# A two-layer transformer in float32 on one core: squares of the norms summed inside the stage in front, mixers with every convolution tap on VectorE and their first tiles in plain float32

## The reference, cut to what matters

```python
def rmsnorm(x, g):
    xf = xf * lax.rsqrt(jnp.mean(xf * xf, axis=-1, keepdims=True) + EPS)
    return xf.astype(x.dtype) * g
def modulate(x, shift, scale):
    return rms_norm(x) * (1 + scale) + shift
...
def second_block(x, mem, ...):
    for l in range(DEPTH):
        xn = rmsnorm(x, norm_mix[l])
        proj = xn @ w_in[l]                                # 1024 -> 2560
        u_pool, u_conv, u_diff, u_sc, u_mem = jnp.split(proj, IN_SPLITS, axis=-1)
        y_pool = pool_mixer(u_pool, pool_w[l], pool_scale[l])
        y_conv = conformer_conv(u_conv, ...)               # a * sigmoid(gate), 31 taps, layernorm, silu, @ pw
        y_diff = diff_attention(u_diff, ...)
        y_sc = short_conv(u_sc, sconv_w[l])
        y_mem = memory_attention(u_mem, mem, ...)          # kv = rmsnorm(mem, mem_g) @ w_kv
        x = x + rmsnorm(cat, group_norm) @ w_out[l]
        x = x + peer_ffn(rmsnorm(x, norm_ffn[l]), ...)
```

## Time and profile before

| | |
|---|---|
| median of 3 runs | 3560.04 us (3558.72 to 3570.94) |
| the profiled execution | 3564.15 us |
| its span | 3562.8 us |
| mean granted clock of PE | 0.944 of full |
| busy | PE 91%, PEld 78%, DVE 58%, ACT 47%, POOL 6% |

### The profile page before, as it was taken

How to read it: one execution, slowest core, us unless ns; L and a number is a source line. 1 busy time by engine, 2 the same in 40 slices (tenths; PEclk the granted TensorE clock), 3 DMA queues, 4 the chain that set the end, 5 groups by cost and what they waited for, 6 DMA issues and landing times.

```text
span 3562.8 us, 51089 instructions
## 1 busy us (share of the span) xinstructions
PE 3245.5 (91%) x19360; PEld 2768.5 (78%) x19360; DVE 2063.8 (58%) x4132; ACT 1664.8 (47%) x3572; POOL 221.6 (6%) x290
## 2 busy tenths in 40 slices
PE   7998999998899777996899999987699779999999
PEld 4745677786699766985689999987598658999998
DVE  2233433335665665598666666656558876666665
ACT  2244322223654335419755555543451685555554
POOL 0021000000200160000000000006100000000000
PEclk9999899997999787999999999978699999999999
DMA  5402344432156322440355555543053115655554
GB/s 207 177 1 83 128 174 166 151 109 72 48 181 179 108 78 65 149 160 1 105 185 185 187 185 188 185 137 106 12 178 131 65 36 184 189 184 184 189 185 153
DMA packets 135059, 479.91 MB, mean 135 GB/s; under 512 B 15520, under 2 KB 17440, under 8 KB 134048
## 3 DMA queue, kind: packets, MB, share of 16 engines
q1 hardware_dynamic: 132944, 471.26, 40.6%
q10 hardware_dynamic: 1872, 5.38, 0.4%
HBM read 475.53 MB, written 1.05 MB: 134 GB/s over the span
## 4 chain that ended last, share of the span: by engine, by line
PE 84%; DVE 8%; issue 4%; ACT 3%; DMA 1%; SPq 0%; ACTq 0%; DVEq 0%
PE psum L706 14%; PE psum L708 14%; PE psum L707 14%; PE psum L2370 7%; PE psum L2371 7%; PE psum L2372 7%; PE psum L2292 6%; PE psum L2216 4%; PE psum L557 3%; PE psum L999 2%; PE psum L354 1%; PE psum L571 1%; DVE conv_part L1457 1%; DVE w_lo L248 1%; PE psum L1009 1%
## 5 line engine op out<-in xcount | busy, mean ns | idle before, releaser
L248 DVE TENSOR_TENSOR w_lo<-raw,w_hi 128x512 fp32r<-128x512 f32 x1472 | 1005.9, 699 | 821.1 <-ACT w_hi L239 793.7
L239 ACT ACTIVATE w_hi<-raw 128x512 fp32r<-128x512 f32 x1472 | 894.8, 625 | 882.3 <-PE psum L708 495.8
L706 PE MATMUL psum<-x_hi,w_hi 128*128 128x256 f32 x2096 | 604.8, 289 | 30.7 <-DVE w_lo L248 23.4
L707 PE MATMUL psum<-x_lo,w_hi 128*128 128x256 f32 x2096 | 600.6, 287 | 0.0
L708 PE MATMUL psum<-x_hi,w_lo 128*128 128x256 f32 x2096 | 597.2, 285 | 0.0
L706 PEld LDWEIGHTS psum<-x_hi,w_hi 128*128 128x128 f32 x2096 | 401.9, 192 | 43.6 <-DVE w_lo L248 25.7
L2370 PE MATMUL psum<-w_hi,wt_hi 128*128 128x512 f32 x1024 | 407.3, 398 | 6.5 <-DVE wt_lo L2428 6.5
L707 PEld LDWEIGHTS psum<-x_lo,w_hi 128*128 128x128 f32 x2096 | 404.0, 193 | 8.2
L2371 PE MATMUL psum<-w_lo,wt_hi 128*128 128x512 f32 x1024 | 407.0, 397 | 0.0
L2372 PE MATMUL psum<-w_hi,wt_lo 128*128 128x512 f32 x1024 | 407.0, 397 | 0.0
L708 PEld LDWEIGHTS psum<-x_hi,w_lo 128*128 128x128 f32 x2096 | 406.8, 194 | 0.0
(11 more groups left out here) (315 smaller groups left out, 4652.4 us busy)
## 6 DMA issues: line engine op xcount, KB each, us to landing
raw<-in_v SPq DMA_DIRECT2D x256, 512.0 KB, 4.2
raw<-in_u SPq DMA_DIRECT2D x190, 512.0 KB, 3.4
raw<-in_mod_w SPq DMA_DIRECT2D x96, 512.0 KB, 4.2
raw<-in_w_gate_up SPq DMA_DIRECT2D x88, 512.0 KB, 4.8
u_raw<-in_u SPq DMA_DIRECT2D x66, 512.0 KB, 3.5
raw<-in_w_in SPq DMA_DIRECT2D x40, 512.0 KB, 4.0
raw<-in_w_down SPq DMA_DIRECT2D x32, 512.0 KB, 3.6
raw<-in_w_peer SPq DMA_DIRECT2D x32, 512.0 KB, 4.2
```

The source lines that it names most:

```text
L239: self.nc.scalar.activation(self.hi[:, m % 4, :], self.half(m), ACT.Copy).then_inc(self.rounded[m % 4], 1)
L248: self.nc.vector.tensor_tensor(self.lo[:, m % 4, :], self.half(m), self.hi[:, m % 4, :], ALU.subtract).then_inc(self.ready[m % 4], 1)
L706: pe.matmul(out[:, 0:width], hi[:, w], x_hi, start=(c == 0), stop=False)
L707: pe.matmul(out[:, 0:width], hi[:, w], x_lo, start=False, stop=False)
```

## The change

It has three parts.

1. **Squares within the stage in front.** For 8 norms (the four between the halves of the first block's layers and at its end, both mixers' and both PEER norms) ACT squares all chunks, DVE adds squares 0 to 6 into one buffer as they come, and PE sums the total and chunk 7's square alone (`tensor_total`): 2 chunks' worth of matmuls instead of 8. For 6 of them (`early=True`) the squares and adds stand inside the stage in front, after the tile that made the chunk. The mixers' norms wait for each chunk by itself but stand after that stage, and the memory has a norm of its own.
2. **Mixers.** All 31 taps on DVE, spread over the tiles of `first`, `mem_kv` and `second`; no conv on POOL, no join. The gate is a Sigmoid and one product. Tiles 4, 5, 2, 3 of w_in and the 4 memory tiles are plain float32 products straight from `raw` (`PlainProjection`). The memory's root, inverse and spread, the convolution's mean and its layernorm's sums stand between tiles.
3. **Ring.** `ring.limit` keeps ACT and DVE from rounding a mixer's weights ahead before that mixer.

```diff
@@ class Ring
-        while self.scalar_made < min(self.scalar_seen + self.ahead, len(self.halves)):
+        while self.scalar_made < min(self.scalar_seen + self.ahead, self.limit or len(self.halves)):
@@ class InvRms
+    def square(self, c):
+        return self.k.sq[:, 3 if c is None else c % 3, 0:self.sets[0][1]]
+
+    def scalar_tile(self, c):
+        act = self.k.nc.scalar
+        act.wait_ge(*self.ready[c])
+        if c >= 3:
+            act.wait_ge(*self.added.after(max(c - 3, 1)))
+        act.activation(self.square(c), self.sets[0][0][c], ACT.Square).then_inc(self.by_scalar.sem, 1)
+
+    def vector_tile(self, c):
+        if not 0 < c < self.n - 1:
+            return
+        dve, total = self.k.nc.vector, self.square(None)
+        dve.wait_ge(*self.by_scalar.after(c + 1))
+        if c > 1:
+            dve.wait_ge(*self.added.after(c - 1))
+        dve.tensor_tensor(total, self.square(0) if c == 1 else total, self.square(c), ALU.add).then_inc(self.added.sem, 1)
+
+    def tensor_total(self):
...
+        for part, mark in ((None, self.added.after(self.n - 2)), (self.n - 1, self.by_scalar.after(self.n))):
+            pe.wait_ge(*mark)
+            for t in range(width // P):
+                m = pe.matmul(self.sums.tensor[:, 4 * t:4 * t + 1], self.square(part)[:, t * P:(t + 1) * P],
+                              k.ones[:, 0:1], start=(part is None and t == 0), stop=(part is not None),
+                              skip_group_check=True)
+        m.then_inc(self.sums.written.sem, 1)
@@ class Residual
     def scalar(self):
         for t in range(DC):
             self.k.ring.round(2 * len(self.cuts))
+            if self.squares is not None and t > 0:
+                self.squares.scalar_tile(t - 1)
             if self.between is not None:
                 self.between.scalar_between(t)
+        if self.squares is not None:
+            self.squares.scalar_tile(DC - 1)
...
             k.ring.remain(2 * len(self.cuts))
+            if self.squares is not None:
+                self.squares.vector_tile(t - 1)
             dve.wait_ge(*self.full(t))
@@ class PlainProjection(Projection)
+    def tensor(self):
...
+            w = k.ring.take_whole()
+            for c in range(DC):
+                if n == 0 and self.arrive is not None:
+                    pe.wait_ge(*self.arrive[c])
+                m = pe.matmul(use.tensor[:, 0:self.width], w[:, c * P:(c + 1) * P], self.x(c), start=(c == 0),
+                              stop=(c == DC - 1))
@@ class Branches
-        act.activation(self.work[:, 0, :, 0:LAT], self.proj[:, 4:6, :], ACT.Exp, scale=-1.0).then_inc(self.raised.sem, 1)
+        act.activation(self.work[:, 0, :, 0:LAT], self.proj[:, 4:6, :], ACT.Sigmoid).then_inc(self.raised.sem, 1)
...
-        dve.wait_ge(*k.vstep(dve.tensor_scalar(gate, gate, 1.0, None, ALU.add)))
-        dve.wait_ge(*k.vstep(dve.reciprocal(gate, gate)))
@@ hooks of the mixer
+class MixerPlain(Between):    # ACT after tile 2: scalar_gate; DVE after tile 3: vector_gate
+class MixerFirst(Between):
+    def tensor_between(self, n):
+        if n == 5:
+            self.mixer.mem_normed.tensor_spread()
+    def scalar_between(self, n):
+        if n == 2:
+            self.mixer.mem_normed.scalar_root()
+    def vector_between(self, n):
+        self.mixer.branches.vector_taps(2 * n, 2 * n + 2)
+        if n == 3:
+            self.mixer.mem_normed.vector_invert()
+        if n == 6:
+            self.mixer.mem_normed.vector_apply()
+class MixerMemory(Between):   # DVE: taps 16+2n, 17+2n; n >= 2: ring.round(0), ring.remain(0)
+class MixerSecond(Between):   # DVE: taps 24+2n, 25+2n up to 30
+class MixerThird(Between):    # n 0: mean, heads' apply, centre, squares; n 2: the layernorm's sums
@@ Mixer.scalar
+        ring.limit = self.second.first_half
+        self.normed.scalar()
+        self.plain.scalar()
+        self.mem_normed.scalar_squares([])
         self.first.scalar()
+        ring.limit = self.beyond()
@@ Mixer.vector
         self.third.vector()
-        self.branches.vector_join().then_inc(self.joined.sem, 1)
...
-        self.ln.vector([self.centred.after(2)])
+        self.ln.vector_invert()
+        self.ln.vector_apply()
```

More of the change, by code:

```diff
@@ L518, in vector_squares @@
         dve = self.k.nc.vector
+        if self.early:
+            return
         hold(dve, after)
+        if self.ready is not None:
+            for c in range(self.n):
+                self.vector_tile(c)
+            return
         for dst, x in self.squares(dve, 1):
@@ L543, in tensor_sums @@
     def tensor_sums(self, between=None):
+        if self.ready is not None:
+            self.tensor_total()
+            return
         k, pe = self.k, self.k.nc.tensor
@@ L1836, in __init__ @@
         gate, hid = k.sb("gate", [P, 2, LAT], 77824), k.sb("hid", [P, 2, LAT], 79872)
-        self.modulated_ffn = Modulate(k, 1, 3, CTX, LAT, a_hi, a_lo, scaled)
+        self.modulated_ffn = self.out.squares = Modulate(k, 1, 3, CTX, LAT, a_hi, a_lo, scaled, self.out.tile_done, True)
         self.ffn = Ffn(k, 1, CTX, LAT, a_hi, a_lo, hidden_hi, hidden_lo, gate, hid, self.modulated_ffn, [])
         x = [k.hT[:, c, CTX:] for c in range(DC)]
-        self.last = Norm(k, [(x, x, columns(k.gvec[:, 0:8], DC), LAT, P, None)])
+        self.last = self.ffn.down.squares = Norm(k, [(x, x, columns(k.gvec[:, 0:8], DC), LAT, P, None)],
+                                                 ready=self.ffn.down.tile_done, early=True)
+        self.tile_done = [self.last.read_mark(0, c) for c in range(DC)]
         self.done = self.last.done
@@ L1994, in sync, with tensor_mean, scalar_mean, vector_centre @@
         self.out.sync()
+    def tensor_mean(self):
+        pe = self.k.nc.tensor
+        pe.wait_ge(*self.branches.conv_made.after(2))
+        pe.wait_ge(*self.mean.free())
+        for c in range(2):
+            m = pe.matmul(self.mean.tensor[:, 0:LAT], self.k.ones[:], self.conv[:, c, :], start=(c == 0), stop=(c == 1))
+        m.then_inc(self.mean.written.sem, 1)
+    def scalar_mean(self):
+        act = self.k.nc.scalar
+        act.wait_ge(*self.mean.full())
+        act.activation(self.mean_row, self.mean.tensor[:, 0:LAT], ACT.Copy,
+                       scale=1.0 / GW).then_inc(self.mean.read.sem, 1)
+    def vector_centre(self):
+        dve = self.k.nc.vector
+        dve.wait_ge(*self.mean.emptied())
+        for c in range(2):
+            dve.tensor_tensor(self.conv[:, c, :], self.conv[:, c, :], self.mean_row,
+                              ALU.subtract).then_inc(self.centred.sem, 1)
     def tensor(self):
-        k, pe = self.k, self.k.nc.tensor
         self.normed.tensor()
+        self.plain.tensor()
+        self.mem_normed.tensor_sums()
         self.first.tensor()
@@ L2006, in tensor @@
         self.third.tensor()
-        pe.wait_ge(*self.joined.after(1))
-        pe.wait_ge(*self.mean.free())
-        for c in range(2):
-            m = pe.matmul(self.mean.tensor[:, 0:LAT], k.ones[:], self.conv[:, c, :], start=(c == 0), stop=(c == 1))
-        m.then_inc(self.mean.written.sem, 1)
-        self.ln.tensor()
+        self.ln.tensor_spread()
         self.branches.tensor()
@@ L2048, in vector @@
         k, dve = self.k, self.k.nc.vector
-        self.normed.vector(self.start + self.fetch.done)
+        ring = k.ring
+        ring.limit = self.second.first_half
+        self.normed.vector()
+        self.plain.vector()
+        self.mem_normed.vector_squares([])
         self.first.vector()
+        ring.limit = self.beyond()
         self.mem_kv.vector()
-        self.heads.vector_squares(self.first.done + self.tiles_done(10) + self.mem_kv.done)
+        self.heads.vector_squares(self.first.done + self.proj_done + self.mem_kv.done)
         lamp, lam = self.lamp, self.lam
@@ L2448, in __init__ @@
         self.normed = Norm(k, [([xn[:, c, :] for c in range(DC)], x, columns(k.gain(l, G_FFN, 8), DC), LAT, P,
-                                [(x_hi[:, c, :], x_lo[:, c, :]) for c in range(DC)])])
+                                [(x_hi[:, c, :], x_lo[:, c, :]) for c in range(DC)])],
+                           ready=mixer.out.tile_done, early=True)
+        mixer.out.squares = self.normed
         xs = lambda c: (x_hi[:, c, :], x_lo[:, c, :])
@@ L2559, in vector_program @@
         self.setup.vector()
+        self.k.ring.limit = self.layers[0].first.first_half
         self.mod.vector_bias()
```

242 lines of the change are left out of this document (159 added, 83 removed).

## The result

The changed kernel takes 3470.64 us (median of 4 runs, 3467.66 to 3473.11), the kernel before 3561.98 beside it (4 runs, 3558.72 to 3570.94): ratio 0.9745, 95% interval 0.9728 to 0.9762. The forecast was 3470. The profiled execution after took 3467.66 us (span 3466.1).

What follows compares the result with a forecast made beforehand. PE bounds the kernel, 84% of the chain, with DVE pacing the mixers' opening. Savings 61.4 + 7.4 + 8.6 + 13.4 = 90.8 us take 3564.15 to 3473, median forecast 3470 (62%); own range 3455 to 3490, 3445 to 3505 for 8 in 10.

Steps and rivals of the forecast that it cites:

- The bound: PE is 84% of the chain; DVE sets the pace in the 16 weight tiles opening a mixer.
- Early norms: Six norms behind a stage: fewer sum matmuls after the last square save 10.6, 9.6, 2.4, 5.7, 3.8 and 5.0 us.
- 4.42 gives 3.8: First norm in front of PEER: no table load needed, 1/8 of the 4.42 us sum kept, 3.8 us saved.
- the first rival: Uncovered squares and adds inside the stages hold up the weight ring, costing 39 to 45 us: 3512 us; chance 12%.
- Mixers' norms: Both mixers' norms, hT to first matmul: root 4.8 us after hT; 11.8 us saved in the first, 12.5 in the second.
- The 16 tiles: First mixer, first matmul to last memory tile: 62.1 us instead of 69.50, 7.4 saved.
- hole: Behind the four plain tiles PE idles 6.2 us (bounds 2 and 10) while gate and memory squares are made.
- The pace of 3.3 us a tile by DVE: Eight split tiles: DVE's roundings, four taps and half an evacuation take 3.3 us per tile against PE's 2.9; 25 in all.
- the 8.6: Second mixer, first matmul to last memory tile: 8.6 us saved, from 72.60 at a lower clock.
- Behind it: After the memory tiles: 0.5 us lost in second, 1.5 saved by a table load, 5.7 before scores; 6.7 per mixer.
- their contended price: Rival: DVE taps stay at 0.909 us as beside POOL and pace all 16 tap-carrying tiles: 3515 us; chance 8%.
- The clock: Rival: after the norms PE's clock stays up as gaps shrink, winning at most 8 x 1.7 us: 3456 us; chance 13%.

Runs made afterwards that it cites:

- the one with fewer filler products: Changed kernel plus unread TensorE products of ones: five between sum and spread of eight norms, ten behind the spread of three modulated norms; 3473.16 us, ratio 0.9745.

## Why the prediction was right, point by point

**The bound.** That DVE set the pace of the mixer's opening and PE's sums that of the norms was right: in that stretch DVE has gone from 60.79 of 69.50 us to 43.83 of 63.40, and PE from 52.94 to 58.72, so that PE is now the limit there.

**Early norms.** 35.7 by the traces, 33.4 by the trace of the kernel with the old sums and 35 by its median, 37.1 forecast. The mechanism is shown twice: late squares lose 30 of it, doubled squares nothing. The table load as what is late next stands in the chain, and the third norm, cut only to it, gave 2.3 for 2.4. Mis-sized is the first norm before PEER ("4.42 gives 3.8"), 2.2: a load of the next stage's weights came late and held up their rounding, and the last square and the last add to hT are queued behind it.

```profile
1369.54 0.63 ACT L239 ACTIVATE w_hi<-raw 128x512 fp32r<-128x512 f32 x1 [2.09 <-DMA raw<-in_w_peer]
```

This is not the first rival, in which squares hold up the rounding: here the rounding waited for a DMA, and two loads of `in_w_peer` took 6.0 us each from issue to landing where the same two took 4.3 and 4.7 in the second mixer. In nine other kernels with early squares and no filler in front of the sums, the stretch was 4.8 to 5.6 us eight times and 6.5 once, against 6.7 here. So the term would mostly have come out at 3.3 to 4.2, near the 3.8; its 2.2 is an accident of this execution, and why the loads were slow in it is open.

**Mixers' norms.** 11.4 and 12.6 for 11.8 and 12.5. The adds took 0.51 each (0.5 taken), the sum 1.8 (1.7), the root stands 5.0 us behind hT (4.8).

**The 16 tiles.** 63.3 and 61.8 us for the 62.1 forecast. The parts: four plain tiles 16.5 and 15.5 (15.8), hole 6.2 in both (6.2), eight split tiles 26.4 and 26.0 (25), memory 14.05 (14.3, and 0.8 of waiting that did not come). The pace of 3.3 us a tile by DVE was wrong at full clock: a tile took 3.0, PE was busy for 13.40 of 13.40 us and DVE for 11.74. The forecast of 25 does not follow from that pace either: a first tile at half clock (4.8) and seven of 3.3 are 27.9, and only PE's 2.9 a tile gives 25. So this term came near by a step that contradicts its own text. The rest lies in the first split tile, 5.3 us at a clock of 0.50 behind the hole. For the second mixer the 8.6 was given without a sum; it measured 10.6. The taps were taken at 0.44 and took 0.477.

**Behind it.** Forecast 6.7 a mixer, measured 2.3 and 8.5. Third's end to the scores is 7.95 us in both (7.7 forecast, right). The step that failed is "the mean and sums cost PE 1.9 inside third": third became 5.7 and 4.2 us longer, since PE waits 2.2 for a bank that the heads' scaling still holds, and in the first mixer two tiles behind that wait took 7.6 us for 6.1. Against it, `second`'s end to the spread gave 2.2, not 1.5. The rest goes with the clock: the heads' sums and `second` took 6.96 and 14.34 us in the first mixer, 5.14 and 13.43 in the second, the same instructions both times, with a clock of 0.50 from 1224 to 1231 us and of 0.69 from 2381.6 to 2386.7. No run fixed what decides this, so the split between 2.3 and 8.5 stays open.

**The rivals.** The ring was not held up by squares: twice as many cost nothing. The taps stayed clear of their contended price, and that price was real: 947 ns with GpSimd at work. The clock fell as before, and earlier than the gap in front of the stage. Windows around the first norm, three of the changed kernel, then two of the one with fewer filler products:

```profile
373.00:376.00 3.00, 2.48 (x22) 2.35 (x21) 0.81 (x3) 2.23 (x4) 0.00 (x0) 1.00 0.13 52
376.00:379.00 3.00, 2.08 (x8) 1.78 (x8) 0.62 (x3) 0.04 (x1) 0.00 (x0) 0.59 0.00 0
379.00:381.50 2.50, 0.00 (x0) 0.00 (x0) 2.50 (x7) 1.73 (x4) 0.00 (x0) 0.50 0.01 3
```

```profile
373.40:376.80 3.40, 3.40 (x18) 3.40 (x17) 0.61 (x2) 0.41 (x3) 0.00 (x0) 0.50 0.00 0
376.80:379.70 2.90, 2.43 (x22) 2.24 (x21) 2.56 (x7) 1.79 (x4) 0.00 (x0) 1.00 0.01 3
```

It had fallen behind the one-column sums and the wait of 1.29 us, before the gap of 2.73; the filler products did not keep it from falling there, but with them it was back at 1.00 when the stage began. The Trainium skill ("TensorE: Matmul & The Clock Gate", HAM oscillation) has it that gaps bring the clock down and the work behind them starts slow. The trace agrees on the slow start (0.50 from 381.5 us), and only in part on the cause, since with the filler products the clock was 0.50 while PE was drawn busy for 3.40 of 3.40 us. That the slow stretch was free behind the first two modulated norms the prediction did not see. The table load was 1.28 and its dummy began 1.29 after it, so the measured price stands, and the 2.66 that the Trainium skill gives ("ScalarE: Activation LUTs", What ACT_TABLE_LOAD costs) had no part in the result.

The sum, 90.8, met 87.5 in the places that it named; that the median came within 1 us of the forecast owes something to errors that cancel, 1 to 4 us each, with both signs.

## What to carry to other kernels

When a norm closes a stage, make its squares inside that stage and add them up as they come: here 30 of 35 us went when the squares were made after the stage, and only the other 5 when the old products came back as well. A new queue of small steps behind a stage (gate, adds, sums) is a hole that its neighbours could have covered; moving the memory's squares and sums forward between the plain tiles gave a fifth as much again as the whole change. Before buying back a slow clock, look at who feeds TensorE: where it waited for VectorE anyway, the clock was worth nothing.

## What was unexpected of the hardware

Equal code in the opening 165 us ended anywhere within 8.0 us in thirteen executions, so one trace's total is not fit to judge an edit worth a few. GpSimd's work raised VectorE's rounding, an instruction that shares no data with it, from 686 to 927 ns, and left the scaling of the memory, whose second input comes from `psum`, at 470. And the same instructions in two mixers of one execution (heads' sums and `second`) took 21.3 and 18.6 us.
